# When the lower experts' rows of four tiles are loaded and added, and how many identity products TensorE runs at the seam between two layers

## The reference, cut to what matters

```
for l in range(DEPTH):                      # DEPTH = 2
    ... mixer: in_proj, chunk mix, differential attention, merge_out ...
    h = rmsnorm(x, g2);  pg = softmax(h @ r_g);  gi = argmax(pg);  gw = max(pg)
    tw, ti = top_k(softmax(le[group gi]), 2);  tw = tw / sum(tw)
    gates = one_hot(gi * 4 + ti) * gw * tw          # two experts of 16 for each row
    a = silu(h @ w_gate[e]) * (h @ w_up[e]) * gates
    x = x + sum over e of a @ w_down[e]
```

## Time and profile before

| | |
|---|---|
| Profiled execution, its own time | 946.92 us |
| Its span in the trace | 945.1 us |
| Median of three runs (lowest, highest) | 948.57 us (945.51, 951.62) |
| TensorE busy | 900.8 us, 95% of the span |
| VectorE, ScalarE, POOL busy | 400.7, 242.4, 184.5 us |
| DMA | 197.48 MB, mean 209 GB/s |
| Lower loads (L1523), higher loads (L1541) | 10 of each, five per layer |

### The profile page before, as it was taken

One profiled execution on the slowest core, in us unless ns is written; L12 is line 12 of the kernel. 1 busy time (PEld: TensorE's weight loads), 2 busy tenths in 40 slices (PEclk: granted clock), 3 DMA queues, 4 the chain that ended last, 5 costly groups with the idle time before them and its releaser, 6 DMA issues. The chain is left out here.

```text
span 945.1 us, 13505 instructions
## 1 busy us (share of the span) xinstructions
PE 900.8 (95%) x4886; PEld 438.9 (46%) x4886; DVE 400.7 (42%) x1039; ACT 242.4 (26%) x495; POOL 184.5 (20%) x259
## 2 busy tenths in 40 slices
PE   9999999999999999999699999999999999999991
PEld 5444455556546444333454444455564464433330
DVE  2403225667547655111233032357664575641114
ACT  3211256643111021111121023466430111211110
POOL 2233201331201111110115032013312002110101
PEclk9999999999999999999799999999999999999996
DMA  9717004251006899999753070043510178999996
GB/s 346 282 53 276 3 1 140 90 179 46 23 37 242 325 419 415 421 420 388 255 227 89 1 277 1 1 139 90 180 46 22 49 274 328 419 407 419 411 375 244
DMA packets 38619, 197.48 MB, mean 209 GB/s; under 512 B 6520, under 2 KB 6648, under 8 KB 22672
## 3 DMA queue, kind: packets, MB, share of 16 engines
q1 hardware_dynamic: 19456, 136.04, 35.9%
q0 software_dynamic: 14736, 45.72, 14.1%
q10 hardware_dynamic: 4352, 14.76, 4.2%
HBM read 175.16 MB, written 27.79 MB: 215 GB/s over the span
## 5 line engine op out<-in xcount | busy, mean ns | idle before, releaser
L725 PE MATMUL ps<-ring,hT 128*128 128x512 f32 (+4 forms) x1264 | 412.4, 584 | 6.8 <-DMA kc<-in_w 4.1
L725 PEld LDWEIGHTS ps<-ring,hT 128*128 128x128 f32 (+2 forms) x1264 | 156.2, 156 | 217.8 <-issue 214.2
L725 PE MATMUL ps<-ring,cat 128*128 128x512 f32 (+3 forms) x544 | 196.5, 597 | 3.1 <-SPq L171 1.6
L725 PEld LDWEIGHTS ps<-ring,cat 128*128 128x128 f32 (+2 forms) x544 | 71.1, 162 | 91.6 <-issue 89.9
L2171 DVE TENSOR_TENSOR hT<-ps,par 128x512 f32<-128x512 f32 x48 | 31.1, 686 | 130.8 <-PE ps L723 125.3
L666 POOL DMA_INDIRECT y_rows<-hn,isca x24 | 24.8, 1034 | 217.6 <-ACT hn L1508 212.3
L545 POOL TENSOR_TENSOR st<-st,half 128x1 f32<-128x1 f32 (+3 forms) x60 | 63.1, 1052 | 11.3 <-POOL st L543 11.0
L1618 DVE TENSOR_REDUCE st<-sqj 128x8 f32<-128x512 f32 x20 | 13.5, 681 | 111.5 <-ACT sqj L1342 111.4
L543 POOL TENSOR_SCALAR st<-st 128x1 f32<-128x1 f32 (+3 forms) x60 | 14.2, 237 | 232.6 <-DVE st L1618 81.6
L725 PE MATMUL ps<-hT,ring 128*128 128x512 f32 x128 | 57.1, 599 | 0.7 <-DVE tmp L1675 0.7
L1508 ACT COPY hn<-ps 128x1024 f32<-128x1024 f32 x22 | 22.3, 1012 | 86.9 <-PE ps L725 86.9
(11 more groups left out here) (297 smaller groups left out, 1093.0 us busy)
## 6 DMA issues: line engine op xcount, KB each, us to landing
ring<-in_w SPq DMA_DIRECT2D x84, 1024.0 KB, 14.9
kc<-in_w SPq DMA_DIRECT2D x10, 1024.0 KB, 17.0
vc<-in_w SPq DMA_DIRECT2D x10, 1024.0 KB, 16.4
v<-in_w SPq DMA_DIRECT2D x10, 1024.0 KB, 13.4
kva<-in_w SPq DMA_DIRECT2D x10, 1024.0 KB, 16.9
kc<-in_ck POOLq DMA_DIRECT2D x32, 256.0 KB, 3.7
vc<-in_cv POOLq DMA_DIRECT2D x32, 256.0 KB, 3.2
h_rows<-qk ACTq DMA_DIRECT2D x10, 512.0 KB, 2.6
```

The lines of the kernel that those rows point to most:

```text
L725: ins = pe.matmul(out, lhsT, rhs, start=start, stop=stop, skip_group_check=loose)
```

## The change

A function `lows_early(l)` says which tiles' lower rows are loaded in the last slots: in layer 0 only tile 0, in layer 1 (the last) all five as before. In layer 0 the loads of tiles 1 to 4 stand at the seam, each ahead of the same tile's higher rows in ScalarE's queue, and VectorE adds them there, ahead of the same tile's higher rows. They use the same semaphores `early_in`. The identity products at the seam are 14 and no longer 39. The route with extra slots is altered to match: its second load of lower rows is the first for tiles 1 to 4.

```diff
+        def lows_early(l):
+            return range(1 if l + 1 < L else NT)
...
@@ POOL, before the first scatter of an extra slot
-                        for t in range(NT):
+                        for t in lows_early(l):
                             wait(*early_in[t].at("early"))
...
@@ TensorE, start of a layer
                 if l:
-                    keep_busy(39, "I")
+                    keep_busy(14, "I")
...
@@ ScalarE, slot LAST + 1
-                        for t in range(NT):
-                            rows = NROW if t == TP else P
-                            act.dma_start(y_low[0:rows, t, :], y_rows[TOK + PLACE[t] * P:...]).then_inc(*early_in[t].inc("early", by=16))
+                        for t in lows_early(l):
+                            low_load(t, early_in[t].inc("early", by=16))
...
@@ ScalarE, the seam without extra slots
                 def load_high():
                     scattered_mains()
                     for t in range(NT):
+                        if t not in lows_early(l):
+                            low_load(t, early_in[t].inc("early", by=16))
                         high_load(t)
...
@@ VectorE, the last slots
                     for t in LOW_AT.get(n - 1, ()):
+                        if t in lows_early(l):
+                            add_low(t)
+                for t in LOW_AT[NSLOT - 1]:
+                    if t in lows_early(l):
                         add_low(t)
-                for t in LOW_AT[NSLOT - 1]:
-                    add_low(t)
...
```

More of the change, by code:

```diff
@@ L1508, in result, with low_load @@
                     nc.scalar.copy(y_sb[:, b, :], ps[:, 6:8, :].rearrange("p a n -> p (a n)")).then_inc(*read["O"].inc("down", *key))
+                def low_load(t, arrival):
+                    rows = NROW if t == TP else P
+                    act.dma_start(y_low[0:rows, t, :], y_rows[TOK + PLACE[t] * P:TOK + PLACE[t] * P + rows, :]).then_inc(*arrival)
                 for n in range(NSLOT + 1):
@@ L1520, in _ @@
                             act.wait_ge(*y_out[b].at("y", "m", last_slot(b, LAST)))
-                        for t in range(NT):
-                            rows = NROW if t == TP else P
-                            act.dma_start(y_low[0:rows, t, :], y_rows[TOK + PLACE[t] * P:TOK + PLACE[t] * P + rows, :]).then_inc(*early_in[t].inc("early", by=16))
+                        for t in lows_early(l):
+                            low_load(t, early_in[t].inc("early", by=16))
                     if n == NSLOT - 1:
@@ L1552, in load_again @@
                         if t < NT:
-                            n = NROW if t == TP else P
-                            act.wait_ge(*dve_s.at("low", t))
-                            act.dma_start(y_low[0:n, t, :], y_rows[TOK + PLACE[t] * P:TOK + PLACE[t] * P + n, :]).then_inc(*low_in[t].inc("low", by=16))
+                            if t in lows_early(l):
+                                act.wait_ge(*dve_s.at("low", t))
+                                low_load(t, low_in[t].inc("low", by=16))
+                            else:
+                                low_load(t, early_in[t].inc("early", by=16))
                         if t >= 2:
@@ L2228, in add_late @@
                     for t in range(NT):
-                        link(add_rows(t, stat["late"][:, t:t + 1], y_low, low_in[t].at("low")))
+                        link(add_rows(t, stat["late"][:, t:t + 1], y_low, low_in[t].at("low") if t in lows_early(l) else early_in[t].at("early")))
                 def extra_index():
```

## The result

The changed kernel took 939.83 us (median of six executions, 937.59 to 941.15) against 948.30 us for the kernel before in the same session: ratio 0.9910, interval 0.9892 to 0.9928 (95%). Run again later it gave 940.68 us, ratio 0.9929 (0.9906 to 0.9951). The forecast was 941.6 us in 937.8 to 946.2. The profiled execution took 939.67 us with a span of 937.9 us, 7.2 us under the span before.

A forecast was written before the change was run, and what follows sets the result against it. TensorE, busy 95% of the span, was taken as the bound, at the seam by a fill longer than what it fills. 5.4 + 2.0 - 0.5 = 6.9 us off the median 948.57 gave 941.6 us, range 937.8 to 946.2.

The forecast's parts named there:

- Part 1: At the seam, 25 identity products fewer let the first tile's turn start sooner: gain 5.4 us.
- Part 2: In layer 0's last slots, four tiles' lower loads leave and TensorE's two waits go: gain 2.0 us.
- Part 3: At the seam, the four moved loads and adds make nobody wait; thinnest margin 0.4 us, at tile 1's turn.
- Part 4: At the seam, a late clock rise could cost 0 to 2.7 us; 0.5 us charged, including part 3's thin margin.
- (a): The seam's loads or the clock bind, costing 2 us each: gain 3.4 us, time 945.2, chance 0.22.
- (b): The two waits in the last slots stay: gain 4.9 us, time 943.7, chance 0.08.
- (d): Slower: the clock stays low past the fill, over three tiles: 4.1 us more, time 952.7, chance 0.03.
- (c): TensorE stops a third time for instructions before the turn: 1.3 us, at worst 5.4, time 942.9 to 947.0, chance 0.05.
- (e): More gained: emptier DMA queues for scatters and branch fetches, shorter stop: gain 8.5 to 10 us, time 939, chance 0.12.

The follow-up runs named there:

- fill only: The kernel before with 14 identity products for 39 and nothing else: 943.96 us, ratio 0.9960 to the kernel before.
- loads only: The changed kernel with 39 identity products again, so only the loads and adds are moved: 946.38 us, ratio 0.9981 to the kernel before.
- par late: The changed kernel with POOL's load of par in layer 1 issued with that of ws, behind tile 2's root: ratio 0.9923 to the kernel before.
- two pieces held: The changed kernel with SP holding layer 1's first two weight pieces until layer 0's last scatters landed: ratio 0.9949 to the kernel before.

## Why the prediction was right

The forecast gain was 6.9 us; measured were 8.5 and 6.7. Both mechanisms are shown apart, by the run with the fill alone and the run with the loads alone. That the first session gave more than the sum is not the forecast's merit: its profile holds 1.0 us of a shorter stop, which the sum had at nothing and which the second profile does not repeat.

**Part 1, the fill, 5.4 us.** Held in the traces: 5.6 us in the profile of fill only, 6.0 in that of the changed kernel, where the clock rose 3.3 us into the unbroken records (463.13 to 466.4) and not 4.45. The time of fill only, 3.8 us (2.7 to 5.0), lies under it, and why stays open.

**Part 2, the two gaps, 2.0 us.** Held: there in the three profiles with all lower loads early (2.0 to 2.4 us), gone in all others; 1.8 us in time, with a wide interval. The step's size was luckier than its working. I had both pieces land near 445, by their bytes at the full rate of 0.41 MB per us. `kva` took 16.0 us from an issue at 431.50 (17.5 before) and landed at 447.5, 0.7 us ahead of the product at 448.22. In the profile of loads only, `kva` and `kc` landed at 446.1 and 449.6, 0.7 and 1.3 us ahead of their products at 446.81 and 450.91. The full rate was the wrong term: there, from 446 to 449, SP's queue moved 0.14 MB and all queues together 89 GB/s, so the last bytes came slowly though the engines had room. Why, no run shows.

**Part 3, the seam, no wait.** Right, by a wider margin than 0.4 us (about 1.3: the first half of tile 1 was there at 475.6, and TensorE was through with tile 0's last four records at 476.9). I kept the pace of the stretch shared with `par` and had high 2 land 12.8 us behind the first load's issue. It was issued at 464.80 and took 7.1 us, so 8.9 us behind. POOL issues `par` only after ScalarE's signal behind its branch (the row at 468.75), now behind nine issues and not five: 5.8 us behind the first load's issue and not 3.5. A moved instruction shifts also whoever waits for its queue, which I had missed. The longer head start of the loads fits their sooner landing but is not shown to be its cause: with `par` out of the way altogether (the two profiles of par late) high 2 took 7.5 and 7.7 us. What the runs do show is that the pace of 2.3 us a tile was too slow for these loads. The run with both pieces held shows the wait itself (1.29 us) once the loads are slowed. The last tile's higher rows, on which SP holds its third piece, were to land 4.6 us later; they landed 5.3 us later (467.42 + 13.9 = 481.3, before 476.0), and no value row waited.

**Part 4, the clock and margin, 0.5 us.** Not needed: the clock rose inside the fill. The bound of 2.7 us was a fair one: with no fill turn and key rows lost 2.5 us at the low clock, of which 1.3 us were left as a later start of the second tile (0.7 with 8 products). The Trainium skill (TensorE: Matmul & The Clock Gate, Part 1) says the release of the clock differs between executions of one kernel; the profiles of the changed kernel agree, with 3.3 us of unbroken records in the one and 2.2 in the other (463.28 to 465.48).

**The rivals.** (a) did not occur here, but a wait of this kind appears where the loads are slowed (two pieces held). (b) and (d) are excluded. (c) a third stop is in no profile. (e) is near by size in the first session (8.5 for its 8.5 to 10), and its shorter stop was in the first profile (5.7 for 6.7), but not in the second (6.5). The measured gain is 1.6 us over the forecast in the first session and 0.2 under in the second; the two intervals overlap.

## What to carry to other kernels

Filling products should end when the data they wait for are there: compare the last filler's end with the ready time of the next operand, and what lies between is what can be gained. A block of loads has a right place and not only a right size; look for what else the DMA engines carry at the new place, scatters and instructions included, and for which engine passes its branch late because the consuming adds moved. After such a change look which chain ends last now: here the fill and the chain of scatter, load and add of the first tile end within about a microsecond of each other, so less fill or a shorter stop alone brought nothing that could be measured.

## What the runs showed that I had not expected

TensorE's stop behind a branch, put down to "issue", goes with the DMA traffic: 5.1 to 7.3 us in ten profiles with 2 MB of weights issued ahead of it, 3.8 us with 1 MB, 2.9 us with none, 8.6 us with 2 MB and 2.4 MB of row loads (the last three are one profile each). Not all of it does: while TensorE stood between the third identity record and the fourth, 1.27 us before and 1.97 us after, all DMA queues together moved 0 and 4 GB/s. The Trainium skill (Runtime: NRT & Kernel Launch, Instruction fetch mechanics) says that a taken branch whose target the engine does not already hold forces a fetch by DMA before execution goes on; these numbers agree with that, but no run here shows the fetch itself as the cause.
